# Token norm with the last expert's rows added by a one-hot product, and the q/k norm on four partition groups

## What is computed

```python
def rms_norm(x, g):
    y = xf * lax.rsqrt(jnp.mean(xf * xf, axis=-1, keepdims=True) + EPS)
    return (y * g)
q = rms_norm(q, g_q) * (HEAD_DK ** -0.5)
k = rms_norm(k, g_k)
```

```python
return jax.vmap(lambda ib, yb: jnp.zeros((S, D)).at[ib.reshape(-1)].add(yb.reshape(-1, D)))(idx, y)
h = layer_norm(x, ln_emb_g, ln_emb_b)
...
out = jnp.einsum('ble,ed->bld', mix, w_out[i]) + b_out[i]
h = layer_norm(DEEPNORM_ALPHA * h + out, ln1_g[i], ln1_b[i])
```

## Time and profile before

| | us |
|---|---|
| median of 3 runs (2178.2 to 2182.43) | 2180.46 |
| the profiled execution | 2185.76 |
| its span in the profile | 2184.0 |
| TensorE busy | 2071.8 |
| VectorE busy | 1684.9 |
| ScalarE busy | 1066.9 |

### The profile page before, as it was taken

One profiled execution on the slowest core, in us unless ns is written; L12 is line 12 of the kernel. 1 busy time (PEld: TensorE's weight loads), 2 busy tenths in 40 slices (PEclk: granted clock), 3 DMA queues, 4 the chain that ended last, 5 costly groups with the idle time before them and its releaser, 6 DMA issues. The chain is left out here.

```text
span 2184.0 us, 24904 instructions
## 1 busy us (share of the span) xinstructions
PE 2071.8 (95%) x9840; PEld 1603.5 (73%) x9840; DVE 1684.9 (77%) x1714; ACT 1066.9 (49%) x1217; POOL 215.8 (10%) x168
## 2 busy tenths in 40 slices
PE   6999998999997999999999859999999998999998
PEld 4767844777865788888888647888888874588876
DVE  5575157895557899999999777999999977864776
ACT  4488134894235677777777522112222167523043
POOL 0200010001000011110110100000000013234040
PEclk9999997999988999999999969999999999899999
DMA  8311171003368999999999741111222245333121
GB/s 304 92 39 39 39 261 43 1 1 90 130 264 338 348 382 400 395 391 400 393 401 392 236 164 42 49 68 40 76 78 97 96 142 187 141 140 116 39 78 58
DMA packets 131071, 381.71 MB, mean 175 GB/s; under 512 B 9580, under 2 KB 22156, under 8 KB 130977
## 3 DMA queue, kind: packets, MB, share of 16 engines
q1 hardware_dynamic: 117184, 340.41, 40.9%
q0 software_dynamic: 7568, 23.09, 4.3%
q10 hardware_dynamic: 6224, 16.93, 1.9%
HBM read 337.28 MB, written 43.06 MB: 174 GB/s over the span
## 5 line engine op out<-in xcount | busy, mean ns | idle before, releaser
L2473 DVE SCALAR_TENSOR_TENSOR arena<-arena,vecs 128x1023 f32<-128x1023 f32 (+14 forms) x240 | 304.4, 1268 | 7.1
L2049 DVE TENSOR_TENSOR w_low<-W,w_high 128x2048 fp32r<-128x2048 f32 x96 | 216.9, 2286 | 34.2 <-ACT w_high L1970 34.2
L2049 DVE TENSOR_TENSOR w_low<-arena,w_high 128x2048 fp32r<-128x2048 f32 x96 | 218.4, 2289 | 19.3 <-ACT w_high L1970 19.3
L1822 PE MATMUL Q<-hT_high,w_high 128*128 128x512 f32 (+1 forms) x736 | 230.0, 392 | 1.3 <-PEq L1842 1.3
L1822 PE MATMUL Q<-hT_low,w_high 128*128 128x512 f32 (+1 forms) x720 | 225.0, 390 | 0.0
L1970 ACT ACTIVATE w_high<-arena 128x2048 fp32r<-128x2048 f32 x96 | 184.2, 1919 | 74.1 <-PE Q L1888 74.1
L1822 PE MATMUL Q<-hT_high,ring_low 128*128 128x512 f32 x704 | 219.9, 390 | 0.0
L1970 ACT ACTIVATE w_high<-W 128x2048 fp32r<-128x2048 f32 x96 | 184.0, 1919 | 69.3 <-PE Q L1888 65.6
L1835 ACT ACTIVATE w_high<-W 128x1024 fp32r<-128x1024 f32 x44 | 46.6, 1059 | 256.1 <-PE Q L1822 243.0
L1888 PE MATMUL Q<-w_high,x_high 128*128 128x512 f32 x512 | 160.9, 396 | 2.4 <-DVE x_low L2052 2.4
L1822 PEld LDWEIGHTS Q<-hT_high,w_high 128*128 128x128 f32 (+1 forms) x736 | 135.4, 184 | 33.2 <-issue 1.8
(11 more groups left out here) (466 smaller groups left out, 4139.9 us busy)
## 6 DMA issues: line engine op xcount, KB each, us to landing
arena<-in_w_dram SPq DMA_DIRECT2D x48, 2048.0 KB, 12.3
W<-in_w_dram SPq DMA_DIRECT2D x48, 2048.0 KB, 13.2
W<-in_w_mod_dram SPq DMA_DIRECT2D x12, 2048.0 KB, 13.3
W<-in_w_in_dram SPq DMA_DIRECT2D x12, 2048.0 KB, 9.2
W<-in_w_out_dram SPq DMA_DIRECT2D x6, 2048.0 KB, 10.8
spill<-arena ACTq DMA_DIRECT2D x24, 512.0 KB, 2.6
W<-in_w_in_dram SPq DMA_DIRECT2D x8, 1024.0 KB, 8.8
arena<-spill SPq DMA_DIRECT2D x3, 2048.0 KB, 10.8
```

The source lines that it names most:

```text
L1822: ins = nc.tensor.matmul(Q[rows, 2 * pair_of(n) + half, :], w[:, k], x[:, k, HALF * half:HALF * half + HALF], start=k == 0 and w is high a ...
L2049: nc.vector.tensor_tensor(wl[:], chunk_src(r, j), wh[:].bitcast(F32), ALU.subtract).then_inc(low_v, 1)
L2473: ins = nc.vector.scalar_tensor_tensor(conf[:, i, j:], u[:, 0:S - j], w, conf[:, i, j:], ALU.mult, ALU.add)
```

## The change

In the q/k norm the mask has 32 columns, eight vectors four times over, and each quarter of the 1024 tokens goes to another 32 partitions: the sums of q or k are one 128 x 256 tile. Root, reciprocal and the parts work on that shape. The partitions' upper half of each 16 holds a copy from which the low part is made, with a column `lower` of ones and zeros and `sign`. The spread mask is the transposed sum mask (four transposes, a new wait `mask_tr`) and spans 128 partitions. TensorE spreads q between the sums of k, and VectorE's norms of q stand between its copies of the biases.

In the token norm the first four tiles (`PICKED`) load before the last scatter, as soon as the scatter before it has landed. TensorE adds the last expert's rows: an identity product of the tile and a product of a one-hot matrix (`picked`) with `y_e`, into PSUM. ScalarE writes (x - mean) / std from there, VectorE multiplies by the gain alone, and the shift is added in the transposed tile by a product of one row with ones behind each transpose. The shift of the untransposed rows goes with `b_out`: a row `row_sum` = ALPHA * shift + `b_out` is made, stored and read in place of `b_out` by the last block. The last scatter waits until the four tiles are loaded.

```diff
-        qk_sum = tiles(5)[:, 0:HEADS * VECS].rearrange("p (b r) -> p b r", b=HEADS)
+        QUARTER, REPEAT = S // 4, P // VECS
+        qk_sum = tiles(4)[:, 0:HALF].rearrange("p (b r) -> p b r", b=HEADS)
...
-                        for half in range(2):
-                            ins = nc.tensor.matmul(Q[rows_of(g), sum_bank[g] + half, :], qk_sum[:, b],
-                                                   tiles(n % 2)[:, HALF * half:HALF * half + HALF],
+                        for q in range(4):
+                            ins = nc.tensor.matmul(Q[32 * q:32 * q + 32, sum_bank[g], 0:QUARTER], qk_sum[:, b, 0:32],
+                                                   tiles(n % 2)[:, QUARTER * q:QUARTER * q + QUARTER],
                                                    start=b == 0, stop=b == HEADS - 1)
                         ins.then_inc(sum_mm, 1)
                         if b % 2:
                             next_vector(2 * g + b // 2)
+                        if g and b:
+                            spread(b - 1)
...
-                    nc.vector.reciprocal(qk_rows[rows_of(g)], qk_rows[rows_of(g)]).then_inc(rows_inv, 1)
+                    nc.vector.reciprocal(qk_rows[:, g], qk_rows[:, g]).then_inc(rows_inv, 1)
+                    dve.wait_ge(rows_inv, g + 1)
+                    nc.vector.tensor_scalar_mul(qk_lower, qk_rows[:, g], lower).then_inc(qk_lower_ready, 1)
...
+                    for q in range(4):
+                        at = slice(32 * q, 32 * q + 32)
+                        ins = nc.vector.scalar_tensor_tensor(
+                            qk_parts[at, QUARTER * q:QUARTER * q + QUARTER], qk_high[at, 2 + g].bitcast(F32),
+                            sign[at], qk_lower[at], ALU.mult, ALU.add)
...
-                sync.wait_ge(*low_level(E, 1))
-                sync.dma_start(emb_b, bc_row(A["ln_emb_b_2"], D)).then_inc(vec_in, 16)
+                sync.wait_ge(*low_level(E, 3))
+                sync.dma_start(b_row, A["ln_emb_b_2"].rearrange("(o n) -> o n", o=1)).then_inc(rows_b_in, 16)
+                sync.dma_start(bo_row, A["b_out_2"][0].rearrange("(o n) -> o n", o=1)).then_inc(rows_b_in, 16)
+                sync.wait_ge(h_tr, E)
+                sync.wait_ge(y_added, 16 * (E - 1))
+                for t in range(PICKED):
+                    sync.dma_start(xt[t], tokens_acc[P * t:P * t + P]).then_inc(xt_in[t], 16)
+                sync.wait_ge(row_sum_ready, 1)
+                sync.dma_start(row_sum, b_sum).then_inc(row_stored, 16)
+                sync.wait_ge(emb_sum, PICKED)
                 sync.wait_ge(y_added, 16 * E)
-                for t in range(NT):
+                for t in range(PICKED, NT):
...
+                def token_sum(t):
+                    pe.wait_ge(xt_in[t], 16)
+                    if t >= 2:
+                        pe.wait_ge(emb_scaled, t - 1)
+                    for n in range(2):
+                        nc.tensor.matmul(Q[:, 4 + 2 * (t % 2) + n, :], ident[:], xt[t][:, HALF * n:HALF * n + HALF],
+                                         start=True, stop=False)
+                    if t == 0:
+                        pe.wait_ge(picked_ready, 1)
+                        pe.wait_ge(y_ready, E)
+                    for n in range(2):
+                        ins = nc.tensor.matmul(Q[:, 4 + 2 * (t % 2) + n, :], picked[:, t],
+                                               y_e[:, HALF * n:HALF * n + HALF], start=False, stop=True)
+                    ins.then_inc(emb_sum, 1)
...
+                token_sum(0)
+                pe.wait_ge(rows_b_in, 32)
                 for t in range(NT):
+                    if t + 1 < PICKED:
+                        token_sum(t + 1)
                     pe.wait_ge(emb_ready, t + 1)
...
-                        ins = nc.tensor.transpose(Q[:, 2 * (t % 2) + k // 4, P * (k % 4):P * (k % 4) + P],
-                                                  xt[t][:, P * k:P * k + P], ident[:])
+                        turned_k = Q[:, 2 * (t % 2) + k // 4, P * (k % 4):P * (k % 4) + P]
+                        nc.tensor.matmul(turned_k, xt[t][:, P * k:P * k + P], ident[:], start=True, stop=False,
+                                         is_transpose=True)
+                        ins = nc.tensor.matmul(turned_k, b_row[:, P * k:P * k + P], ones[0:1, :],
+                                               start=False, stop=True)
...
+                    act.wait_ge(emb_shift, t + 1)
+                    nc.scalar.activation(xt[t], bank2(2 + t % 2) if t < PICKED else xt[t], ACT.Identity,
+                                         bias=shift_col[t % 2], scale=rstd[:, t:t + 1]).then_inc(emb_scaled, 1)
...
+                dve.wait_ge(rows_b_in, 32)
+                nc.vector.scalar_tensor_tensor(b_sum, b_row, ALPHA, bo_row, ALU.mult, ALU.add).then_inc(row_sum_ready, 1)
                 outputs(E - 1, pair=0)
                 low_part2(dve, 1)
                 stats(0)
...
+                    if isinstance(e, int) and e == E - 1:
+                        for t in range(PICKED):
+                            pool.wait_ge(xt_in[t], 16)
...
-                for dst, v in ((b_out, A["b_out_2"][0]), (ln1_g, A["ln1_g_2"][0])):
+                for dst, v in ((b_out, row_sum[0]), (ln1_g, A["ln1_g_2"][0])):
```

More of the change, by code:

```diff
@@ L955, in _ @@
                 pe.wait_ge(masks, 2)
+                for b in range(HEADS):
+                    ins = nc.tensor.transpose(Q[:, 7, P * b:P * b + P], qk_sum[:, b], ident[:])
+                ins.then_inc(mask_tr, 1)
                 sums(0)
@@ L959, in _ @@
                 next_vector(4)
-                pe.wait_ge(masks, 7)
-                pe.wait_ge(mask_ready, 1)
-                spread(0)
+                spread(HEADS)
+                spread(HEADS + 1)
                 row_product(5)
-                spread(1)
+                spread(HEADS + 2)
+                spread(HEADS + 3)
             @block.scalar
@@ L1058, in _, with far @@
                 invert(0)
+                dve.wait_ge(sign_ready, 1)
+                low_rows(0)
                 added(2)
-                low_rows(0)
                 dve.wait_ge(near_ready, HEADS)
-                for h in range(HEADS):
+                def far(h):
                     nc.vector.tensor_copy(bias_all[:, h, 0:6 * P], bias_near[h][:, 0:1].broadcast_to((P, 6 * P)))
@@ L1066, in _ @@
                                           bias_near[h][:, HALF - 1:HALF].broadcast_to((P, 6 * P)))
+                far(0)
+                for n in range(HEADS - 1):
+                    norm(n)
+                    far(n + 1)
                 added(3)
+                norm(HEADS - 1)
                 invert(1)
+                low_rows(1)
                 added(4)
-                norm(0)
-                low_rows(1)
-                for n in range(1, HEADS):
-                    norm(n)
+                norm(HEADS)
+                norm(HEADS + 1)
                 added(5)
-                for n in range(HEADS, 2 * HEADS):
-                    norm(n)
+                norm(HEADS + 2)
+                norm(HEADS + 3)
         TURNS = HEADS * NT
@@ L1650, in norm_stats @@
             v_link(nc.vector.bn_aggr(mv[:, 0:2], bn[:, 0:12]))
-        xt = [tiles(t) for t in (0, 1, 2, 3, 4, 5, 6, 13)]
+        xt = [tiles(t) for t in (0, 1, 2, 4, 5, 6, 3, 13)]
         stack = arena[0:VROWS, 10 * 1024:10 * 1024 + 12 * P]
@@ L1661, in program @@
         emb_T_low = sem("emb_T_low")
+        emb_sum, emb_shift, emb_scaled = sem("emb_sum"), sem("emb_shift"), sem("emb_scaled")
+        rows_b_in, row_sum_ready, picked_ready = sem("rows_b_in"), sem("row_sum_ready"), sem("picked_ready")
+        row_stored = sem("row_stored")
+        shift_col = [lam_tmp[:, 2 + j:3 + j] for j in range(2)]
         emb_stored = sem("emb_stored")
@@ L1947, in _ @@
                             ins = product2(pe, i, i, k, (0,))
-                pe.wait_ge(small2_in, 16 * (4 + NT + 8))
-                for m in range(12):
-                    bank, c0 = 5 + 2 * (m // 6), VROWS * (m % 6)
-                    ins = nc.tensor.transpose(Q[:, bank, c0:c0 + VROWS], stack[:, P * m:P * m + P],
-                                              ident[0:VROWS, 0:VROWS])
-                ins.then_inc(vec_tr, 1)
             @block.scalar
@@ L2019, in _, with emb_high @@
                 high_part2(act, 1)
-                root(0)
-                for t in range(NT):
-                    if t + 1 < NT:
-                        root(t + 1)
+                def emb_high(t):
                     act.wait_ge(emb_tr, t + 1)
```

128 lines of the change are left out of this document (82 added, 46 removed).

## The result

The changed kernel takes 2231.12 us (median of 4 runs, 2229.18 to 2232.62), the kernel before 2181.44 on the same chip (4 runs, 2178.2 to 2186.28): a ratio of 1.0221, 95% interval 1.0206 to 1.0235, so 2.2% slower. The prediction was 2192.5 in a range of 2178 to 2202: right in sign, wrong in size by 39 us. The profiled execution has a span of 2228.9 us, against 2184.0 before.

The account below looks back on a forecast made before the run. It took VectorE to bound the token stage after an 18 us start chain, and the q/k norm's end; token stage +19.5 and q/k norm -7.5 made +12, 2197.8, less 5.3 to the median: 2192.5 us, range 2178 to 2202.

Parts of the forecast that it names:

- the steady part: Token stage after its first transposes: 45.3 us from first to last transposes; stage +5.5 at the high clock throughout.
- Its clock, +14,: Token stage: low clock level for the transposes of tiles 0 to 4 and a third of two sums, +14 us.
- three half products of tiles 4 to 6: Token stage from tile 4 on: twelve half products at 0.23, 2.76 us a tile beside the transposes.
- The start: Token stage: earlier tile loads bring the first transposes to 1262.1 us against 1268.05, -6.0.
- The added wait of VectorE for the two small rows: Token stage start: VectorE waits for two 4 KB rows, moving the last expert's rows from 1250.18 to 1252.2 us.
- The ring: Token stage: transposes, sum of tile t+2, its statistics and gain of t+1 wait in turn, 9.45 us a tile, two turns.
- rival 1: Token stage: clock stays high, +5.5 there and -7.5 in q/k norm, -2 in all, 2178.5 us; chance 0.12.
- q/k norm, -7.5: End of the q/k norm: reshaped reciprocal and norms end at 336.2 us instead of 343.70, so -7.5.
- from 318.7: product 1.9 to 320.6: q/k norm tail: once a last gate weight unit lands at 318.7 us, its product takes 1.9.
- The four small row operations: q/k norm tail: four 32 x 256 row operations on VectorE, not in the trace, taken as 0.35 us each.
- rival 2: Token stage: fp32 identity, one-hot and K=1 products take one pass, stage -5.2, total -13, 2168 us; chance 0.09.
- rival 3: q/k tail held by weights or low clock, gaining only 0 to 3.5; total +16 to +19.5, 2196.5 to 2200 us; chance 0.15.

Follow-up runs that it names:

- e3: Changed kernel with each tile's eight one-row products behind all eight of its transposes instead of alternating with them; 2203.48 us.
- e4: Changed kernel with the shift added by a 128-row product (broadcast shift row times identity) behind each transpose, not a one-row product; 2185.67 us.
- e9: As e4, with VectorE's statistics of the next tile put behind its gain of this tile instead of ahead; 2178.07 us.
- e13: Changed kernel with eight transposes first, then eight shift products of 128 rows behind them in each tile; 2186.13 us.
- e10: As e9, with two tiles instead of four getting the last expert's rows from TensorE; 2178.75 us, ratio 0.9987 to the kernel before.
- e1: Kernel before with the new q/k norm alone, nothing of the token part; 2177.42 us against 2182.01, ratio 0.9976.

## Why the prediction was wrong

**The step that failed** is this one of the steady part: "The transposes now have a K=1 product each, fp32 of 128 columns, two records; such records come every 0.12 us (16 in 1.95) and a transpose likewise. So 24 records, 2.85 us a tile high, 5.7 low." The number of records was right. The price was taken from rows in which records of one shape follow one another and put on records that alternate between 128 rows and one. A pair costs 0.68 high and 1.13 low, a tile 5.4 and 9.1. With one row kept together (e3) or 128 rows kept throughout (e4, e9) the predicted price comes out: e9 has 2.83 us a tile high, and e3 5.4 to 5.7 low.

**Its clock, +14,** failed in part. I had the low level for tiles 0 to 4, 40 pairs. Measured, tile 0 is low (9.1), tile 1 partly (7.5), tiles 2 to 4 take 27.1 us back to back, all low with TensorE busy throughout, tile 5 is high (5.4), and tiles 6 and 7 are low in part (7.1 and 7.0): 42 pairs wholly low, 19 wholly high, 3 between. The number of low pairs came out right, in part by luck: I named idle time and one-row products together and let the level recover behind tile 4, but tiles 2 to 4 are low with no idle time in them, and the level falls again in tiles 6 and 7. The low level in the half products between the tiles was put at nothing, and too little of it stood in the sums. Over the whole stage the granted clock is 0.66 in the changed kernel and 0.88 in e4, which differs by the rows alone.

The account of the token stage, from TensorE's timeline, in us:

| term | predicted | measured |
|---|---|---|
| first transposes behind the last expert product | 12.0 | 12.0 |
| eight tiles of transposes with the shift, clock included | 22.8 + 14.2 = 37.0 | 63.1 |
| sums of tiles 2 and 3 | 7.0 + 2.6 = 9.6 | 11.9 |
| three half products of tiles 4 to 6 | 3 x 2.76 = 8.3 | 14.3 |
| twelve transposes of vectors | 0.95 | 1.5 |

The last four rows are 35 us over, and the stage is 34 over (53.5 less 19.5). At the predicted prices, 0.71 and 0.36 a pair, the measured mix of levels would have taken some 38 us (an estimate: 42 x 0.71 + 19 x 0.36 + 3 x 0.53). So of the 26.1 in the second row some 25 are the changes of rows, 8.8 in the rows below are the low level, and the pairs that were low beyond the forecast are about 1. In the experiments, putting the one-row products behind one another took 30 us off the stage (e3), and 128 rows in their place took off another 13 (e13 against e3); both figures hold what the clock gave back.

**What held.** The start, to a tenth. The added wait of VectorE for the two small rows: 7.74 us idle before L2204, and the last expert's rows at 1245.77, where the sum gave 1252.2 less what the q/k norm brings. An identity and one-hot sum of 3.6 us high (predicted 3.5); at the low level its first half took 3.57, so 7.1 for a whole one (predicted 7.0). The ring: its turns are 17.4 and 16.4 us with transposes and sums at their measured lengths, instead of 9.45. Nothing came back later. That e9 and e10 stand at 2178, the time of rival 1, is luck: they have another order on VectorE. With the order of the change and 128 rows (e4) the time is 2185.67, some 7 above that rival.

**q/k norm, -7.5.** Right in mechanism, 1.7 too large: -5.8 at the attention's start. The term "from 318.7: product 1.9 to 320.6" is the one off: its product started at 319.42 and took 2.90, so it ended at 322.3, 1.7 later. The four small row operations took 0.49 each, not 0.35. In whole runs the part is worth 4.6 (e1).

**The rivals.** Rival 1 needed one-row products that don't touch the clock, rival 2 single records, rival 3 a q/k norm that gives nothing; none came. The cited rule that a VectorE copy between groups doesn't break warmth (the Trainium skill, "TensorE: Matmul & The Clock Gate", "Loop structure matters more than you think") holds here only in part. In e9, with 128 rows throughout, the pairs behind waits for VectorE of 1.57 and 0.93 us ran at the high level, but those behind one of 2.88 us took 0.64, the low level; in e4 the pairs behind two waits of 2.72 us began low too. It says nothing on few rows, which decide here. The pair was priced too low and the clock in part, and a bound above the sum was missing: for the K=1 product, which was not in the trace, I bounded from below (one record) but took the dearest row that I had as the upper end. The row to ask was the earlier trace rows, 303 to 306 us, where the clock fell to 0.54 in a TensorE busy for 100% of the time beside products with 32 rows. I used it to argue the sign of the clock and not its size.

## What to carry to other kernels

Price an instruction of TensorE by the shape of its neighbours, not only its own: count the changes between 128 rows and fewer, and either put all few-row products of a tile behind one another or fill them up to 128 rows. Here the first took 30 us off the stage, the second 40, for the same sums. Early loads of a few tiles behind the scatter before the last were worth having; moving VectorE's shift to TensorE was not, in any version measured: the version with the two old passes on VectorE is the fastest (2171.4), and the best with the shift on TensorE has 2178.

## What the hardware showed that I had not expected

A change between 128 rows and 1, 32 or 64 rows cost 0.24 us at the low level and 0.17 at the high one, the same for the three, and the weight load behind it was not made ahead. The granted clock didn't follow the busy share: with 64 rows in the shift products it stayed at 0.50 over 16.8 us of TensorE's work without a gap, while with 128 rows it was 0.77 over the same work with TensorE busy for 81% of it.
